# The last MLP's down product by seven block products, and the final norm by tokens

## The reference

```
def sq_relu_mlp(hn, w1, w2):
    return jnp.square(jax.nn.relu(hn @ w1)) @ w2
...
        h = h + sq_relu_mlp(rmsnorm(h, norm_mlp_g[l]), mlp_w1[l], mlp_w2[l])
...
    return rmsnorm(h, final_norm_g)
```

## Time and profile before

| | before |
|---|---|
| median of 3 runs | 1999.28 us (1997.5 to 2000.58) |
| profiled execution, first to last instruction | 1997.9 us |
| TensorE busy | 1979.0 us, 99% |
| VectorE busy | 1162.7 us, 58% |
| ScalarE busy | 765.1 us, 38% |
| GpSimd busy | 244.6 us, 12% |
| last chain of waits | TensorE 94%, VectorE 3% |

### The profile page before, as it was taken

The page is one execution under the profiler, slowest core; times in us unless marked ns, Lnnn a source line. Parts: engine busy times, 40 slices in busy tenths (PEclk is TensorE's granted clock), DMA queues, the critical chain, the costliest instruction groups (busy, mean ns, idle before and its releaser), DMA issues.

```text
span 1997.9 us, 23010 instructions
## 1 busy us (share of the span) xinstructions
PE 1979.0 (99%) x9333; PEld 1624.3 (81%) x9333; DVE 1162.7 (58%) x1673; ACT 765.1 (38%) x1206; POOL 244.6 (12%) x189
## 2 busy tenths in 40 slices
PE   9999999999999999999999999999999999999998
PEld 7877777888888888888888888888877778888887
DVE  6665687577665656647677444443587674333334
ACT  5453554344333333533324323223554353232224
POOL 1001340000000000000001132221221012222221
PEclk9999999999999999999999999999999999999999
DMA  5322212113232323323222323323232013323321
GB/s 177 108 79 85 85 63 85 64 64 101 89 106 85 106 87 103 106 93 98 87 83 89 106 90 101 104 87 105 74 86 98 24 43 106 105 85 106 103 87 64
DMA packets 138713, 180.51 MB, mean 90 GB/s; under 512 B 9712, under 2 KB 97392, under 8 KB 138608
## 3 DMA queue, kind: packets, MB, share of 16 engines
q1 hardware_dynamic: 136720, 177.52, 27.2%
q10 hardware_dynamic: 1632, 1.51, 0.2%
q0 software_dynamic: 256, 0.02, 0.0%
HBM read 176.91 MB, written 2.10 MB: 90 GB/s over the span
## 4 chain that ended last, share of the span: by engine, by line
PE 94%; DVE 3%; ACT 1%; issue 1%; DMA 0%; POOL 0%; SPq 0%; ACTq 0%; POOLq 0%; DVEq 0%
PE bank L529 26%; PE bank L531 25%; PE bank L530 25%; PE bank L693 4%; PE bank L572 2%; PE bank L574 2%; PE bank L573 2%; PE bank L685 1%; PE bank L783 1%; PE bank L771 1%; PE bank L998 1%; DVE w_lo L1153 1%; DVE arena L1192 1%; PE bank L775 1%; ACT h_hi L1926 0%
## 5 line engine op out<-in xcount | busy, mean ns | idle before, releaser
L529 PE MATMUL bank<-h_hi,w_hi 128*128 128x512 f32 x1384 | 545.7, 394 | 2.0 <-DVE w_lo L1153 2.0
L531 PE MATMUL bank<-h_hi,w_lo 128*128 128x512 f32 x1384 | 539.8, 390 | 0.0
L530 PE MATMUL bank<-h_lo,w_hi 128*128 128x512 f32 x1384 | 539.4, 390 | 0.0
L1911 ACT ACTIVATE w_hi<-raw 128x1024 fp32r<-128x1024 f32 (+2 forms) x335 | 331.1, 1031 | 498.8 <-PE bank L531 442.7
L529 PE MATMUL bank<-g_hi,w_hi 128*128 128x512 f32 (+1 forms) x972 | 377.2, 388 | 1.4 <-issue 0.7
L531 PE MATMUL bank<-g_hi,w_lo 128*128 128x512 f32 (+1 forms) x972 | 371.9, 383 | 0.0
L530 PE MATMUL bank<-g_lo,w_hi 128*128 128x512 f32 (+1 forms) x972 | 371.5, 382 | 0.0
L499 POOL TENSOR_TENSOR w_lo<-raw,w_hi 128x1024 fp32r<-128x1024 f32 (+1 forms) x75 | 182.1, 2429 | 1490.8 <-ACT w_hi L1911 1490.8
L1153 DVE TENSOR_TENSOR w_lo<-raw,w_hi 128x1024 fp32r<-128x1024 f32 (+2 forms) x258 | 309.0, 1221 | 60.8 <-ACT w_hi L1911 59.9
L1215 DVE TENSOR_TENSOR resid<-bank,resid 128x512 f32<-128x512 f32 x287 | 194.3, 688 | 224.9 <-PE bank L531 224.1
L529 PEld LDWEIGHTS bank<-h_hi,w_hi 128*128 128x128 f32 x1384 | 260.3, 188 | 58.4 <-issue 2.8
(11 more groups left out here) (241 smaller groups left out, 1796.0 us busy)
## 6 DMA issues: line engine op xcount, KB each, us to landing
raw<-w SPq DMA_DIRECT2D x64, 1024.0 KB, 5.2
raw<-w_up SPq DMA_DIRECT2D x22, 1024.0 KB, 5.0
raw<-a_w_in SPq DMA_DIRECT2D x16, 1024.0 KB, 5.3
raw<-w_in SPq DMA_DIRECT2D x11, 1024.0 KB, 5.3
raw<-w_down SPq DMA_DIRECT2D x11, 1024.0 KB, 5.0
raw<-w_mkv SPq DMA_DIRECT2D x8, 1024.0 KB, 5.3
raw<-a_w_out SPq DMA_DIRECT2D x8, 1024.0 KB, 5.0
raw<-w_out SPq DMA_DIRECT2D x4, 1024.0 KB, 5.1
```

Source lines behind the costliest of these rows:

```text
L529: nc.tensor.matmul(dst, a_hi, b_hi, start=(k == 0), stop=False)
L530: nc.tensor.matmul(dst, a_hi, b_lo, start=False, stop=False)
L531: last = nc.tensor.matmul(dst, a_lo, b_hi, start=False, stop=(k == n - 1))
L1911: A(hi, src, ACT.Copy).then_inc(w_hi_done, 1)
```

## The change

The down product of the last MLP is made token-major by Strassen's scheme. In each of eight granules of 512 hidden features the left operand (512 tokens x 512 features) is cut into 2 x 2 blocks of 256 x 256 (A11, A12 for the first 256 tokens; in the code a11, a21, a12, a22 are views of `last_g`), the weights into 2 x 2 blocks of 256 x 512 (b11, b12, b21, b22 in `quarters`). Seven products of block sums take the place of eight. GpSimd makes the four sums of weights T1 to T4 in place over the blocks (T2 in `second_form`), and the four sums S1 to S4 of the left operand (`last_s`); ScalarE and VectorE split each weight form and each left form into halves.

The order of the products is P1, P2, P6, P4, P7, P5, P3. A granule has eleven weight pieces of 1024 columns: p to p+3 are the two chunks of `w1`, p+4 to p+10 the weight forms of the seven products in their order (B11, B21, T2, T4, T3, T1, B22). `w_hi` and `w_lo` are now a ring of four such pieces, so a piece can be made when the piece four before it has been used. P1 and P2 stay in PSUM banks of their own over all granules; the other products are added to sums in SBUF by VectorE in each granule. In granules 1 to 4 TensorE transposes the residual into those sums, eight transposes in each, between the two chunks of `w1`. In the last granule VectorE puts the sums together (`together`), and P6 and P7 use P1's banks.

The final norm is by tokens: ScalarE squares the blocks with a sum over the row, takes the root, VectorE inverts it, ScalarE and VectorE scale, and eight stores of 128 x 512 go out.

```diff
+        PRODUCTS = ("P1", "P2", "P6", "P4", "P7", "P5", "P3")
+        A_GRANULE = 4 + len(PRODUCTS)
+        FORM_OF = {"P1": "B11", "P2": "B21", "P6": "T2", "P4": "T4", "P7": "T3", "P5": "T1", "P3": "B22"}
...
+        def low_by_pool(p):
+            return p % A_GRANULE == A_GRANULE - 1 or (p % A_GRANULE == 0 and p > 0)
...
+            for n in range(GRANULES):
+                p = A_GRANULE * n
+                if n:
+                    low_piece(p)
+                wait_lows(pool, p + 5)
+                pool.wait_ge(quarter_loaded[1], 16 * (n + 1))
+                G.tensor_tensor(b11, b12, b11, ALU.subtract).then_inc(form_made, 1)
+                pool.wait_ge(form_made, 4 * n + 1)
+                G.tensor_tensor(second_form, b22, b11, ALU.subtract).then_inc(form_made, 1)
+                wait_lows(pool, p + 6)
+                pool.wait_ge(form_made, 4 * n + 2)
+                G.tensor_tensor(b21, second_form, b21, ALU.subtract).then_inc(form_made, 1)
+                pool.wait_ge(g_made, 4 * n + 2)
+                pool.wait_ge(left_ready, 7 * n)
+                G.tensor_tensor(s3, a11, a21, ALU.subtract).then_inc(left_made, 1)
+                G.tensor_tensor(b12, b22, b12, ALU.subtract).then_inc(form_made, 1)
+                pool.wait_ge(left_made, 4 * n + 1)
+                pool.wait_ge(g_made, 4 * n + 4)
+                G.tensor_tensor(s2, a22, s3, ALU.subtract).then_inc(left_made, 1)
+                G.tensor_tensor(s1, a21, a22, ALU.add).then_inc(left_made, 1)
+                pool.wait_ge(left_made, 4 * n + 2)
+                G.tensor_tensor(s4, a12, s2, ALU.subtract).then_inc(left_made, 1)
+                low_piece(p + 10)
...
-            mlp()
...
+            def product(n, j):
...
+                wait_lows(pe, p + 1)
+                pe.wait_ge(left_ready, 7 * n + (1, 3, 4, 5, 5, 6, 7)[j])
...
+                for t in range(2):
+                    dst = (on[t] if kept else next_bank())[:]
+                    cut = slice(P * t, P * t + P)
+                    for k in range(2):
+                        begin = opens and k == 0
+                        nc.tensor.matmul(dst, a_hi[:, k, cut], b_hi[:, k, :], start=begin, stop=False, skip_group_check=kept)
+                        nc.tensor.matmul(dst, a_hi[:, k, cut], b_lo[:, k, :], start=False, stop=False, skip_group_check=kept)
+                        last = nc.tensor.matmul(dst, a_lo[:, k, cut], b_hi[:, k, :], start=False,
+                                                stop=k == 1 and (ends or not kept), skip_group_check=kept)
...
+            for n in range(GRANULES):
+                last_up(n, 0)
+                for half, t in jobs_of(n):
+                    turn_tokens(half, t)
+                last_up(n, 1)
+                for j in range(len(PRODUCTS)):
+                    product(n, j)
...
+                rectified(0)
+                rectified(1)
+                low_piece(p + 4)
+                low_piece(p + 5)
+                low_left("P1", last_g[:, 0:2, 0:256], hi + 2)
+                for half, t in jobs_of(n):
+                    take_tokens(half, t)
+                if ends:
+                    together(sums["P7"], sums["P7"], sums["P6"], ALU.add)
+                    together(sums["P3"], sums["P3"], sums["P6"], ALU.add)
+                rectified(2)
+                low_left("P7", left_sum(2), hi + 3)
...
+                rectified(3)
+                low_left("P2", last_g[:, 2:4, 0:256], hi + 5)
...
+                square_tile(0)
+                high_piece(p + 4)
+                square_tile(1)
+                high_piece(p + 5)
+                act.wait_ge(left_made, 4 * n + 1)
+                high_left("P7", 2)
+                tile.n += len(jobs_of(n))
+                square_tile(2)
+                square_tile(3)
+                high_piece(p + 6)
+                act.wait_ge(left_made, 4 * n + 2)
+                wait_used(act, p + 4, start_last)
+                high_left("P6", 1)
```

More of the change, by code:

```diff
@@ new lines, in up_loads, with lows_by_vector, lows_by_pool, wait_lows @@
+        def up_loads(c):
+            return loads[(OLD + c) % 2] + 16 * (c // 2 + 1)
+        def low_by_pool(p):
+            return p % A_GRANULE == A_GRANULE - 1 or (p % A_GRANULE == 0 and p > 0)
+        def lows_by_vector(pieces):
+            return by_vector(OLD) + sum(not low_by_pool(p) for p in range(pieces))
+        def lows_by_pool(pieces):
+            return by_pool(OLD) + sum(low_by_pool(p) for p in range(pieces))
+        def wait_lows(engine, pieces):
+            engine.wait_ge(w_split, lows_by_vector(pieces))
+            if lows_by_pool(pieces) > by_pool(OLD):
+                engine.wait_ge(w_split_pool, lows_by_pool(pieces))
@@ L383, in build, with ring, left_form @@
+        def ring(t, p):
+            return t[:, p % 4 // 2, 1024 * (p % 2):1024 * (p % 2) + 1024]
+        def left_form(t, product):
+            tiles, first = LEFT_OF[product]
+            return t[:, tiles, first:first + 256]
         block = ctx.enter_context(nc.Block())
@@ L409, in _ @@
                     sp.dma_start(dst, src).then_inc(w_loaded[c % 2], 16)
[L411 to L418, removed]
+            up_cols = w["w1_1"].rearrange("(k p) n -> p k n", p=P)
@@ L1874, in _ @@
[L1874 to L1883 removed]
+            sum_squares(sq, KT)
@@ new lines, in _ @@
+            low_left("P5", left_sum(0), hi + 7)
+            for t in range(2):
+                take(lambda b: V.tensor_tensor(sums["P4"][:, t, :], sums["P4"][:, t, :], b[:], ALU.subtract))
+            low_piece(p + 9)
+            low_left("P3", left_sum(3), hi + 8)
+            dve.wait_ge(tile_taken, tile.n)
+            dve.wait_ge(kept_full, first_kept + 4)
+            for t in range(2):
+                V.tensor_tensor(sums["P4"][:, t, :], KEPT["P1"][t][:], sums["P4"][:, t, :], ALU.add).then_inc(y_ready, 1)
@@ new lines, in _ @@
+            for t in range(2):
+                keep_order(V.tensor_tensor(turned_last[:, t, :], KEPT["P1"][t][:], turned_last[:, t, :], ALU.add))
+            dve.wait_ge(kept_taken, 2)
+            first = tile.n
+            for t in range(2):
+                dve.wait_ge(tile_full, first + t + 1)
+                if t == 0:
+                    settle()
+                V.tensor_tensor(turned_last[:, t, :], tile_bank[(first + t) % 4][:], turned_last[:, t, :], ALU.add)\
+                 .then_inc(y_ready, 1)
+                take(lambda b: V.tensor_tensor(sums["P3"][:, t, :], b[:], sums["P3"][:, t, :], ALU.add))
@@ L1961, in down @@
                 for n in range(KT):
[L1962 to L1971 removed]
+                    if last:
                         taken()
@@ L2347 @@
+            for half, y in ((1, sums["P4"]), (0, turned_first)):
+                act.wait_ge(y_inv, 2 - half)
+                for t in range(2):
+                    act.wait_ge(y_gained, 4 if half else 2)
+                    A(y[:, t, :], y[:, t, :], ACT.Copy, scale=rstd_col[:, 2 * half + t:2 * half + t + 1]).then_inc(out_scalar, 1)
 def kernel(**inputs):
```

394 lines of the change are left out of this document (301 added, 93 removed).

## The result

The changed kernel takes 2051.39 us, median of 4 runs (2050.27 to 2052.14), against 1999.28: a ratio of 1.026 [1.0246, 1.0275]. The change costs 52 us. The profiled execution spans 2048.5 us.

The account below looks back on a forecast made before the run. TensorE's work was taken to bound the kernel before; after the change, stalls in the chain. 1637.85 + 52.1 + 6 x 47.4 + 66.6 = 2040.9 us of span, with 1.4 for the median 2042; range 2022 to 2062.

Parts of the forecast that it names:

- The likeliest case: Last MLP: P2 waits in every granule behind the chain and the GpSimd/VectorE exclusion; 2028 to 2055 us, 62 in 100.
- the second slow case: TensorE's clock falls in the gaps ahead of P2, on top of the stalls: 2054 us, 22 in 100.
- The chain and the exclusion: Each granule: VectorE and GpSimd instructions reading two SBUF inputs wait for each other's end; P2 stalls 5.2 us.
- the step on the transposes: Granules 1 to 4: the residual's transposes on TensorE fall into the stall, so their 3.7 us cost nothing more.
- the rival at 2001: Last MLP: the chain alone delays P2, GpSimd and VectorE not excluding each other; granules of 42.4 us, 8 in 100.
- the rival at 1979: Last MLP: GpSimd's sums come early enough, P2 starts within 0.5 us of P1's end; faster, 8 in 100.
- the rival at 2054: P2's 12 matmuls run at 1.2 GHz after each gap: 1.5 us a granule, 12 in all; 22 in 100.
- P6's wait: Each ordinary granule: P6 waits for its left low and starts at 33.65 instead of 32.4, 1.2 us more.
- P2 of granule 0: First granule: rstd comes late, so P2 starts at 1672.25; the granule takes 52.1 us.
- the MLP's start: TensorE's first up matmul of the last MLP was put at 1637.85, with 0.94 us for the statistic.
- The tail: Behind the last matmul: final additions, norm, scalings and stores, 9.5 us instead of 10.8.
- the ordinary granule: Granules 1 to 6 take 47.4 us each instead of 40.8, through the waits of TensorE.

Follow-up runs that it names:

- e2: The changed kernel with GpSimd's eight sums a granule replaced by memsets of about the same length that read no SBUF, output not the reference's: 2010.86 us.
- e4: The changed kernel with the eight sums a granule made by VectorE, GpSimd keeping only its two low pieces: 2004.72 us.
- e6: The changed kernel with GpSimd's eight sums a granule cut to 8 columns, same waits and order, output not the reference's: 1990.08 us.
- e3: The changed kernel with spare matmuls ahead of P2 that fill TensorE's wait, their result not used: 2046.79 us.
- e1: The changed kernel with GpSimd making S3 ahead of T1 instead of behind T4: 2042.82 us.
- e7: e1 with GpSimd's two low pieces a granule moved to VectorE: 2023.8 us.
- e9: e5 with VectorE making GpSimd's two low pieces as well, so GpSimd is left out of the stage: 1989.65 us.
- e5: e4 with the last granule's six additions spread and its low of p+9 ahead of VectorE's takes of P4: 1997.26 us.

## Why the prediction was right

The forecast was 2042 us, range 2022 to 2062, and slower with 0.84; measured 2051.39. The likeliest case came true, with the mechanism of the second slow case on top of it. By its own steps:

**The chain and the exclusion: right, to 0.2 us.** Granule 5, in us from its first up matmul at 1881.18, predicted and measured: T1 begins 13.47 and 13.54; T2 ends 19.18 and 19.27; T4 21.96 and 22.07; S3 23.36 and 23.32; the low of S3 26.38 and 26.21; tile 3 rectified 27.0 and 26.82; S2 29.03 and 29.17; the left low of P2 29.58 and 29.73; P2 starts 29.7 and 29.87, with a gap of 5.2 and 5.23. The waits of whole instructions are in the rows above, and e2 shows by itself that it isn't GpSimd's being busy that holds VectorE: instructions as long that only write do so far less. In granules 1 to 4 the gap is 4.06 us beside 0.9 us of transposes, as the step on the transposes said: they fall into the stall.

**The chain without the exclusion (the rival at 2001): false here, as in e2's groups.** Its number is near what e2 (2010.86) and e4 (2004.72) gave, since these take the meetings, or most of them, away.

**The scheme pays (the rival at 1979): false for this placement.** With sums that take next to nothing (e6) it pays 10 us, not 20: the last granule keeps gaps of 5.5 us, and granules 1 to 6 take, the transposes aside, some 0.75 us more than 40.8 each.

**The clock falls in the gaps (the rival at 2054): it happened in every gap ahead of P2, and its size was put too high.** It was costed at 1.5 us a granule, 12 in all; e3 puts it at 4.6. I had let all 12 matmuls of P2 run slow. In granules 0 to 4 only 6 or 7 did, 1.3 us, which P6's wait of 1.2 takes up; 13 of granule 5, 10 of granule 6 and those of granule 7 cost more. The interval from P2 to P2 shows it, in us: 48.10, 47.97, 47.89, 47.89, 48.06 and then 49.19, against 47.4 predicted. The Trainium skill (TensorE: Matmul & The Clock Gate, What's actually happening) has the throttled state as the default that activity releases; the traces agree that idleness brings the fall (no fall in e3, where it is filled), and the rule says nothing of what else waits meanwhile, which set the size.

**Where the 9.4 us come from.** In the span 7.6: P2 of granule 0 started at 1671.14, 1.1 earlier than the 1672.25 put down. Of that 0.66 is the MLP's start: its first up matmul stands at 1637.19, and in the kernel before at 1637.39, not at 1637.85, since the statistic costs TensorE 1.4 us there and not 0.94 (the matmul behind it takes longer too). Six intervals took 289.1 us instead of 284.4, +4.7. From P2 of granule 6 to that of granule 7 it was 55.4 instead of 54.0, +1.4. From there to the end of the matmuls (2039.3) it was 23.7 instead of 20.8, +2.9. The tail was 9.2 instead of 9.5, -0.3. The other 1.8: the median lies 2.9 us above this execution's span, where it was 1.4 before (0.3 are rounding); the profiled execution was the fastest of the four, at 2050.27. So the largest mis-sized term is the ordinary granule, at 47.4 instead of about 48.2, and then the last one. The clock is only part of the first: e3, at full clock, still has 47.8 from P2 to P2. There P6's wait is about as costed (1.05 us against 1.2), and P3 starts 3.0 us behind P5, where the chain had 2.75; the rest lies in steps of 0.1 us.

**What the prediction didn't see** is in e1: it named S3 as the place that decides, and putting S3 right gave 8.6 us, not 29. Behind it stood a second meeting of the same kind, at the end of the granule, which the prediction had at 0.1 us (P5 behind the lows that wait for GpSimd's p+10 and p+11) and e7 took away for 19 us. And e9 is a way that it didn't weigh: it took GpSimd's share as given, where leaving GpSimd out is 7.6 us faster than keeping only its two low pieces (e5).

**What stays open.** The 11.8 us ahead of the last P2 stay 11.6 in e1 and e7 and fall to 7.0 in e4 and to 0 in e5, which fits the six additions, met by GpSimd's sums. The first two additions in the changed kernel and in e4:

```profile
1998.94 5.65 DVE L2065 TENSOR_TENSOR arena<-arena 128x1024 f32<-128x1024 f32 x2
```

```profile
1962.67 2.48 DVE L2043 TENSOR_TENSOR arena<-arena 128x1024 f32<-128x1024 f32 x2
```

With the additions where the changed kernel has them the gap is 6.6 us in e2 and 2.4 in e6, so GpSimd's sums are the larger part of it. The additions were not moved alone.

Of the 21.8 us of matmuls that the scheme saves, e9 shows 8.4 in the span (1997.9 to 1989.5). 3.7 are the transposes that moved in front, and 4.7 gaps (0.42 and 2.51 in granule 0, 1.78 in the last). The other 5 its trace shows too: the MLP starts 1.05 us later in this execution (1638.44 against 1637.39), the matmuls at the lower clock in granule 0 cost 1.4, and steps of up to 0.2 us ahead of P2 and P6 make the rest, some 2.6 over granules 1 to 7. Behind the last product both kernels take 10.9 us, so the tail saves nothing there.

## What to carry to other kernels

Work given to an idle GpSimd isn't free when VectorE has instructions with two SBUF inputs: each meeting costs one of them what is left of the other's instruction, and busy totals (here 17% and 65%) don't show it. Read the stretched rows, and price a chain across engines by each engine's program order; when one stall is taken out, the next one stands right behind it (e1, e7). A scheme that saves a few per cent of matmuls has to be paid for at the start and the end of the stage too, where nothing covers the chain.

## What the runs showed that I had not expected

- Leaving an engine out was the best use of it: GpSimd idle in the stage 1989.65 us (e9), with two low pieces a granule 1997.26 (e5).
- A GpSimd memset of 2722 columns runs for 2.38 us beside VectorE's two-input instructions without holding them as sums of the same length do (e2: left lows 831 ns on average, against 1636).
- The same gap can bring the clock down or not. TensorE in e5 and in e9, P2 of granule 0:

```profile
1667.18 0.47 PE L1259 MATMUL bank<-w_hi,g_hi 128*128 128x512 f32 x1 [2.51 <-DVE g_lo L2013]
```

```profile
1667.18 0.77 PE L1254 MATMUL bank<-w_hi,g_hi 128*128 128x512 f32 x1 [2.51 <-DVE g_lo L2008]
```

The first goes on at full clock, the second with slow matmuls, after 2.51 us of idleness in both. Shorter gaps did either as well: behind 1.95 us in granule 5 of e1 and 1.96 us in granule 5 of e2 eight matmuls ran at the lower clock, from the fifth on in e1 and from the third on in e2, and behind 1.95 and 1.96 us in e7 none did.
